# Rotary swap by transfers of SyncE and GpSimd, second tile of V normed later, turns of the identity behind the columns

## The chip, the cores and the metric

The kernel runs on one core of a Trainium2 chip. A core has a matmul engine (TensorE, PE), a vector engine (VectorE, DVE), an activation engine (ScalarE, ACT), GpSimd (POOL) and SyncE (SP), which work at the same time and wait for one another by semaphores. Data lies in on-chip memory (SBUF, 128 partitions), matmul results in eight banks of PSUM. Transfers are issued from an engine's queue and run on 16 DMA engines. The metric is the device time of one execution, in microseconds (us); a tuned kernel counts as faster or slower only where runs of both differ by more than they scatter.

## What is computed

A block of two transformer layers, then a block with another kind of attention, over 256 tokens of width 1024, batch 1, all in float32. Each of the two layers is a gated feed-forward, a mixer and a second feed-forward, with a layer norm behind each. The change touches the mixer, whose core is (cut from the reference):

```python
z = x @ w_in
u, v, q, k, val, gates = jnp.split(z, SPLITS, axis=-1)
u = jax.nn.gelu(u, approximate=False)
v = jax.nn.gelu(v, approximate=False)
h_a = _chunked_sgu(u, v, sgu_ln_g, sgu_ln_b, sgu_w, sgu_b)   # layer norm of v, causal matmul over time, times u
q = _rope(q.reshape(...), cos, sin)
k = _rope(k.reshape(...), cos, sin)
...
def _rope(x, cos, sin):
    x1, x2 = jnp.split(xf, 2, axis=-1)          # halves of 32 channels in each head half of 64
    return jnp.concatenate([x1 * c - x2 * s, x2 * c + x1 * s], axis=-1)
```

The rotary embedding needs, for each channel, its partner 32 channels away. Channels lie on partitions here, so this is a swap of partitions p and p ^ 32. The second block takes time vectors through a modulation (`silu(c) @ w_mod + b_mod`), of which some parts are computed between the steps of the first block.

## The kernel before

Every weight matrix is streamed once. SyncE loads chunks of 1 MB into a ring of three tiles `raw` (function `load`, L634 on; a chunk is loaded when both low halves of the chunk three before it are made). A chunk has two parts of 128 x 1024. For each part ScalarE makes a rounded high half `whi` (L1408) and VectorE, or at layer norms GpSimd, the low half `wlo` = raw - whi (L1861, L2425), in rings of four. A product is then three matmuls (high x high, high x low, low x high), and the order of making halves is that of class `Weights`: `take` makes what is up to four parts ahead, `pass_by(1)` passes one part, `more(k)` makes k parts ahead if the ring has room.

`gemm_a` (L716, L717, L719) has the weights stationary and 256 tokens moving: 8 x 3 = 24 matmuls for a block of 128 output channels. `gemm_b` (L739, L741, L742) has the tokens stationary and 512 weight columns moving.

A mixer goes: the V part by `gemm_b` (8 weight parts), then 16 query and key blocks by `gemm_a` (n = 0 to 15), the gating matmuls (L923, the layer-normed V times the causal matrix), 8 U blocks, then the value part, gates with attention woven in, branches and output.

The rotary, for block n: ScalarE copies the bank to the tile s of the ring `mtmp` (four tiles, L1490). TensorE, one block later, multiplies it by a permutation matrix `perm` into bank 4 or 5 (`rotate`, L904). VectorE multiplies that by the sine into the tile u of the ring (L1974) and s by the cosine into Q or K (L1975). GpSimd adds both (L2484). The order on each engine is that in which its function is written:

```python
                for n in range(16):
                    b = n % 4
                    empty(b)
                    gemm_a(bank[b][:, 0:T], xt, ("qk", l, n))
                    emptied[b] = ((AMX, ("qk", l, n)),)
                    if n:
                        rotate(n - 1)
```

VectorE norms V's two tiles (L1957 to L1967) ahead of these blocks, with GpSimd's power for 1/sqrt (L2477). It adds the bias to the gating result into SG (L1986), which uses banks 6 and 7 in turn.

`mod_columns` (L826) turns a row of the modulation into columns with eight small instructions (four matmuls of 2 columns). `modulation` does the same from sums that VectorE makes, and has one transpose of the identity matrix behind it (`settle`, L774), written to an unused part of the bank, which then carries the signal.

## Time and profile before

| | us |
|---|---|
| median of 3 runs | 1823.71 (1823.33 to 1826.53) |
| the profiled execution | 1826.43 |
| its span | 1824.7 |
| TensorE busy (share of the span) | 1789.1 (98%) |
| VectorE busy | 1136.3 (62%) |
| ScalarE busy | 866.2 (47%) |
| GpSimd busy | 249.4 (14%) |

The span is the time from the first to the last instruction in the profile; 1.7 us lie around it. Matmuls overlap, so the length of one (0.28 us) is more than the time to the next one's start. A transfer is not counted as an engine's busy time.

### The profile page before, as it was taken

The numbers are of one execution on the slowest core, as the hardware profiler recorded it, in microseconds if no ns is written. First come the engines' busy times: TensorE is split into PE (matmuls) and PEld (weight loads), VectorE is DVE, ScalarE is ACT, GpSimd is POOL, SyncE is SP. The second block draws the span as 40 slices with busy tenths as digits, with TensorE's granted clock in tenths as the row PEclk, the third lists the DMA queues.
The fourth block names the chain that finished last, engine by engine and source line by source line (L and its number), as shares of the span: only waits on it lengthen the run. The fifth ranks groups of instructions, "written<-read, shape, count | busy, mean of one in ns | idle before, by whom it ended". The sixth has DMA issues, their size and how long they took to land.

```text
span 1824.7 us, 31051 instructions
## 1 busy us (share of the span) xinstructions
PE 1789.1 (98%) x12824; PEld 1618.3 (89%) x12824; DVE 1136.3 (62%) x1735; ACT 866.2 (47%) x1412; POOL 249.4 (14%) x264
## 2 busy tenths in 40 slices
PE   9999999999999999999999999999999899999998
PEld 8998699999899879997899997999787777889998
DVE  5764686686666466656675776566645555655553
ACT  5453344664445435443435753545345345445443
POOL 2000232121200020002321212000111343100000
PEclk9999999999999999999999999999999999999999
DMA  8565654446566666755745455675553333355553
GB/s 289 188 229 191 227 185 162 162 139 198 195 205 211 208 205 227 238 186 173 260 150 182 140 185 196 222 234 184 172 171 91 95 90 107 116 172 181 188 188 105
DMA packets 252397, 330.58 MB, mean 181 GB/s; under 512 B 13162, under 2 KB 213072, under 8 KB 252256
## 3 DMA queue, kind: packets, MB, share of 16 engines
q1 hardware_dynamic: 248240, 315.31, 53.0%
q0 software_dynamic: 4016, 13.27, 2.1%
q8 instruction: 102, 1.67, 0.4%
q14 instruction: 39, 0.32, 0.0%
HBM read 327.51 MB, written 1.05 MB: 180 GB/s over the span
## 4 chain that ended last, share of the span: by engine, by line
PE 62%; issue 24%; DVE 6%; POOL 3%; ACT 2%; DMA 2%; SPq 0%; POOLq 0%; DVEq 0%; ACTq 0%
PE bank L716 14%; PE bank L719 14%; PE bank L717 14%; PE bank L739 4%; PE bank L741 4%; PE bank L742 4%; DVE X L1939 1%; DMA G<-in_lam_dram 1%; DVE wlo L1861 1%; PE bank L1278 1%; ACT whi L1408 1%; POOL rs L2459 1%; PE bank L1256 1%; PE bank L904 1%; PE bank L942 1%
## 5 line engine op out<-in xcount | busy, mean ns | idle before, releaser
L1861 DVE TENSOR_TENSOR wlo<-raw,whi 128x1024 fp32r<-128x1024 f32 x537 | 664.2, 1241 | 383.6 <-ACT whi L1408 379.7
L1408 ACT ACTIVATE whi<-raw 128x1024 fp32r<-128x1024 f32 x549 | 574.2, 1051 | 390.5 <-PE bank L742 166.1
L716 PE MATMUL bank<-XTh,whi 128*128 128x256 f32 x1984 | 559.9, 282 | 0.0
L719 PE MATMUL bank<-XTh,wlo 128*128 128x256 f32 x1984 | 551.1, 278 | 0.0
L717 PE MATMUL bank<-XTl,whi 128*128 128x256 f32 x1984 | 550.8, 278 | 0.0
L716 PEld LDWEIGHTS bank<-XTh,whi 128*128 128x128 f32 x1984 | 373.4, 188 | 2.9
L717 PEld LDWEIGHTS bank<-XTl,whi 128*128 128x128 f32 x1984 | 374.0, 189 | 1.0
L719 PEld LDWEIGHTS bank<-XTh,wlo 128*128 128x128 f32 x1984 | 372.8, 188 | 0.4 <-DVE wlo L1861 0.3
L716 PE MATMUL bank<-HCh,whi 128*128 128x256 f32 (+1 forms) x880 | 252.4, 287 | 0.6 <-DVE tmp L2355 0.6
L717 PE MATMUL bank<-HCl,whi 128*128 128x256 f32 (+1 forms) x880 | 248.3, 282 | 0.0
L719 PE MATMUL bank<-HCh,wlo 128*128 128x256 f32 (+1 forms) x880 | 248.2, 282 | 0.0
L716 PEld LDWEIGHTS bank<-HCh,whi 128*128 128x128 f32 x880 | 166.1, 189 | 15.7 <-issue 11.4
L717 PEld LDWEIGHTS bank<-HCl,whi 128*128 128x128 f32 x880 | 164.9, 187 | 1.8
L719 PEld LDWEIGHTS bank<-HCh,wlo 128*128 128x128 f32 x880 | 164.8, 187 | 1.7
L2459 POOL TENSOR_TENSOR rs<-rs,half 128x1 f32<-128x1 f32 x12 | 18.3, 1525 | 650.7 <-DVE rs L1933 650.7
L741 PE MATMUL bank<-wlo,ffn1Hh 128*128 128x512 f32 x264 | 102.7, 389 | 0.0
L739 PE MATMUL bank<-whi,ffn1Hh 128*128 128x512 f32 x264 | 102.7, 389 | 0.0
L742 PE MATMUL bank<-whi,ffn1Hl 128*128 128x512 f32 x264 | 102.7, 389 | 0.0
L739 PE MATMUL bank<-whi,XTh 128*128 128x512 f32 x192 | 75.2, 391 | 0.0
L741 PE MATMUL bank<-wlo,XTh 128*128 128x512 f32 x192 | 74.8, 389 | 0.0
L742 PE MATMUL bank<-whi,XTl 128*128 128x512 f32 x192 | 74.7, 389 | 0.0
L742 PEld LDWEIGHTS bank<-whi,ffn1Hl 128*128 128x128 f32 x264 | 49.6, 188 | 10.3
(344 smaller groups left out, 2425.7 us busy)
## 6 DMA issues: line engine op xcount, KB each, us to landing
raw<-in_ffn_w_dram SPq DMA_DIRECT2D x131, 1024.0 KB, 5.1
raw<-in_w_in_dram SPq DMA_DIRECT2D x76, 1024.0 KB, 5.0
raw<-in_w_mod_dram SPq DMA_DIRECT2D x24, 1024.0 KB, 5.1
raw<-in_w_branch_dram SPq DMA_DIRECT2D x16, 1024.0 KB, 4.9
raw<-in_w_out_dram SPq DMA_DIRECT2D x12, 1024.0 KB, 4.8
raw<-in_w_ffn_gate_dram SPq DMA_DIRECT2D x11, 1024.0 KB, 5.2
raw<-in_w_ffn_up_dram SPq DMA_DIRECT2D x11, 1024.0 KB, 5.1
raw<-in_w_ffn_down_dram SPq DMA_DIRECT2D x8, 1024.0 KB, 5.2
```

The source lines that it names most:

```text
L716: e.matmul(o, hi[:, k, w0:w0 + nc_], xh, start=first and k == 0, stop=False)
L717: e.matmul(o, hi[:, k, w0:w0 + nc_], xl, start=False, stop=False)
L719: m = e.matmul(o, lo[:, k, w0:w0 + nc_], xh, start=False, stop=last and k == nk - 1)
L739: e.matmul(o[:, :], xh, hi[:, k, s], start=kk == 0, stop=False)
L741: e.matmul(o[:, :], xh, lo[:, k, s], start=False, stop=False)
L742: m = e.matmul(o[:, :], xl, hi[:, k, s], start=False, stop=kk == nparts * nk - 1)
L904: e.matmul(bank[b][:, 0:T], perm, mtmp[tm[l].slot["s", n]][:, :], start=True, stop=True).then_inc(SMALL.did(("perm", l, n)), 1)
L942: e.matmul(bank[b][:, 0:256], Q[r, h, 128:256], K[r, h, :], start=True, stop=True)
L1256: e.matmul(bank[b][:, :], QNT[r, h // 2, t * 128:(t + 1) * 128], KNT[r, h // 2, :], start=True, stop=True).then_inc(SMALL.did(("ns", u)), 1)
L1408: e.activation(hi_part(n), raw_part(n), ACTF.Copy).then_inc(WHI.did(n), 1)
L1861: e.tensor_tensor(lo_part(n), raw_part(n), hi_part(n).bitcast(F32), ALU.subtract).then_inc(WLO.did(n), 1)
L2459: e.tensor_tensor(rs[:, t, 1:2], rs[:, t, 0:1], nhalf, ALU.pow).then_inc(PLN.did(("rs", j, t)), 1)
```

## The change

- The permutation matrix and its 16 matmuls a layer go. For each block, two transfers on SyncE's queue (rows 0 to 63 of the tile) and two on GpSimd's (rows 64 to 127) copy 32 rows each of s to the swapped place in u. SyncE issues those of two blocks behind each of eight loads; GpSimd's stand in its own loop.
- VectorE multiplies u by the sine in place, in SBUF, two blocks behind the product (`times_sin`), the cosine one block behind. The ring `mtmp` has eight tiles in place of four, and each block its own s and u.
- `norm_v(1)` and GpSimd's power for it are written behind the first query block; ScalarE's and VectorE's `more(1)` ahead of it goes. The loads of the next norm's parameters on GpSimd move to the sixth block.
- `mod_columns` has a turn of the identity behind it, and one stands ahead of the first query block.
- The constants lose 128 columns, so the tiles behind them lie 512 bytes lower.

```diff
--- before.py
+++ after.py
...
-    chunks, on_dve = [], {}
+    chunks, on_dve, first_qk = [], {}, []
...
+        first_qk.append(len(chunks))
...
+        ROT = [signal(f"s_rotary{i}") for i in range(4)]
+        ROTP = [signal(f"s_rotary_pool{i}") for i in range(4)]
...
-        cm, cos, sin, perm = csa[:, 0:256], csa[:, 256:512], csa[:, 512:768], csa[:, 768:896]
+        cm, cos, sin = csa[:, 0:256], csa[:, 256:512], csa[:, 512:768]
...
-            mtmp = some(st, "mtmp", 4, [128, T])
+            mtmp = some(st, "mtmp", 8, [128, T])
...
         tm = []
         for l in range(2):
-            r = Ring(4)
+            r = Ring(8)
             for n in range(16):
-                r.use(("s", n), (SMALL, ("perm", l, n)), (DMX, ("cos", l, n)))
-                if n:
-                    r.use(("u", n - 1), (PMX, ("rot", l, n - 1)))
+                r.use(("s", n), (ROT[n % 4], ("turned", l, n)), (ROTP[n % 4], ("turned", l, n)), (DMX, ("cos", l, n)))
+                r.use(("u", n), (PMX, ("rot", l, n)))
             for n in range(8):
                 r.use(("g", n), (XLO, ("ha", l, n)))
-                if n == 0:
-                    r.use(("u", 15), (PMX, ("rot", l, 15)))
             for n in range(8):
@@ -647,6 +646,15 @@
                 cs = hs[j][1]
                 e.dma_start(dst[:, :, cs], src[:, :, cs]).then_inc(FIRST[j].did(j, by=16), 16)
 
+            def turned(l, n):
+
+
+                ring_free(q, tm[l], ("u", n))
+                q.wait_ge(AMX, ("qk", l, n))
+                for p in (0, 32):
+                    e.dma_start(mtmp[tm[l].slot["u", n]][p:p + 32, :], mtmp[tm[l].slot["s", n]][p ^ 32:(p ^ 32) + 32, :]).then_inc(
+                        ROT[n % 4].did(("turned", l, n), by=16), 16)
+
...
             for c in range(1, before_bias):
                 load(c)
+                for l in range(2):
+                    if first_qk[l] <= c - 4 < first_qk[l] + 8:
+                        for j in range(2):
+                            turned(l, 2 * (c - 4 - first_qk[l]) + j)
...
                 for j in range(4):
-                    mm = e.matmul(bank[b][:, 2 * j:2 * j + 2], spare[0:m, j * 128:(j + 1) * 128], cmb[0:m, :], start=True, stop=True)
-                mm.then_inc(MOD.did(("columns", g)), 1)
+                    e.matmul(bank[b][:, 2 * j:2 * j + 2], spare[0:m, j * 128:(j + 1) * 128], cmb[0:m, :], start=True, stop=True)
+                settle(b).then_inc(MOD.did(("columns", g)), 1)
                 emptied[b] = ((DMD, g),)
@@ -897,21 +909,13 @@
                 for b in range(4, 8):
                     emptied[b] = ((AMX, ("V", l, (b - 4) // 2, b % 2)),)
 
-                def rotate(n):
-                    b = 4 + n % 2
-                    q.wait_ge(AMX, ("qk", l, n))
-                    empty(b)
-                    e.matmul(bank[b][:, 0:T], perm, mtmp[tm[l].slot["s", n]][:, :], start=True, stop=True).then_inc(
-                        SMALL.did(("perm", l, n)), 1)
-                    emptied[b] = ((DMX, ("sin", l, n)),)
-
+                empty(3)
+                settle(3)
                 for n in range(16):
                     b = n % 4
                     empty(b)
                     gemm_a(bank[b][:, 0:T], xt, ("qk", l, n))
                     emptied[b] = ((AMX, ("qk", l, n)),)
-                    if n:
-                        rotate(n - 1)
                 for g2 in range(4):
                     b = 6 + g2 % 2
                     q.wait_ge(DMX, ("v", l, 1))
@@ -928,8 +932,6 @@
                     empty(b)
                     gemm_a(bank[b][:, 0:T], xt, ("u", l, n))
                     emptied[b] = ((AMX, ("u", l, n)),)
-                    if n == 0:
-                        rotate(15)
...
@@ -1479,8 +1481,6 @@
                     if t:
                         w.more(3)
                     q.wait_ge(MM, ("V", l, t))
-                    if t:
-                        w.more(1)
                     for c in range(2):
                         e.activation(V[:, t, c * 512:(c + 1) * 512], bank[4 + 2 * t + c][:, :], ACTF.Gelu).then_inc(AMX.did(("V", l, t, c)), 1)
@@ -1949,9 +1949,7 @@
             def mixer(l):
                 w.pass_b(8, 3)
                 w.more(3)
-                for t in range(2):
-                    if t:
-                        w.more(1)
+                def norm_v(t):
                     for c in range(2):
                         q.wait_ge(AMX, ("V", l, t, c))
                         e.bn_stats(st6[:, t, c, :], V[:, t, c * 512:(c + 1) * 512]).then_inc(DMX.did(("stats", l, t, c)), 1)
...
-                def rotate(n):
-                    b, dst, j, scale = 4 + n % 2, (Q, K)[n // 8], n % 8, (0.125, 1.0)[n // 8]
-                    u = mtmp[tm[l].slot["u", n]]
-                    q.wait_ge(SMALL, ("perm", l, n))
-                    ring_free(q, tm[l], ("u", n))
-                    e.scalar_tensor_tensor(u[:, :], bank[b][:, 0:T], scale, sin, ALU.mult, ALU.mult).then_inc(DMX.did(("sin", l, n)), 1)
+                def times_cos(n):
+                    dst, j, scale = (Q, K)[n // 8], n % 8, (0.125, 1.0)[n // 8]
+                    q.wait_ge(AMX, ("qk", l, n))
                     e.scalar_tensor_tensor(dst[:, j, :], mtmp[tm[l].slot["s", n]][:, :], scale, cos, ALU.mult, ALU.mult).then_inc(
                         DMX.did(("cos", l, n)), 1)
 
+                def times_sin(n):
+                    u, scale = mtmp[tm[l].slot["u", n]], (0.125, 1.0)[n // 8]
+                    q.wait_ge(ROT[n % 4], ("turned", l, n))
+                    q.wait_ge(ROTP[n % 4], ("turned", l, n))
+                    e.scalar_tensor_tensor(u[:, :], u[:, :], scale, sin, ALU.mult, ALU.mult).then_inc(DMX.did(("sin", l, n)), 1)
+
+                norm_v(0)
                 for n in range(16):
                     w.pass_by(1)
+                    if n == 0:
+                        norm_v(1)
                     if n:
-                        rotate(n - 1)
+                        times_cos(n - 1)
+                    if n > 1:
+                        times_sin(n - 2)
+                times_cos(15)
                 q.wait_ge(MIN[l], "in")
                 for g in range(8):
...
                 for n in range(8):
                     w.pass_by(1)
-                    if n == 0:
-                        rotate(15)
-                    else:
+                    if n < 2:
+                        times_sin(14 + n)
+                    if n:
                         low("ha", HAl, HAh, n - 1, mtmp[tm[l].slot["g", n - 1]])
                 low("ha", HAl, HAh, 7, mtmp[tm[l].slot["g", 7]])
@@ -2472,29 +2479,43 @@
                                 channel_multiplier=1).then_inc(PMX.did(("ws", l)), 1)
                 w.pass_b(8, 3)
                 w.more(3)
-                for t in range(2):
+
+                def power(t):
                     q.wait_ge(DMX, ("var", l, t))
                     e.tensor_tensor(rs[:, t, 1:2], rs[:, t, 0:1], nhalf, ALU.pow).then_inc(PMX.did(("rs", l, t)), 1)
-                q.wait_ge(DMX, ("v", l, 1))
-                load_gb((2, 6)[l], I["ln_g"][l, 1], I["ln_b"][l, 1])
-
+
+                power(0)
                 def rotate(n):
                     dst, j = (Q, K)[n // 8], n % 8
+                    q.wait_ge(DMX, ("sin", l, n))
                     q.wait_ge(DMX, ("cos", l, n))
                     e.tensor_tensor(dst[:, j, :], dst[:, j, :], mtmp[tm[l].slot["u", n]][:, :], ALU.add).then_inc(PMX.did(("rot", l, n)), 1)
 
+                def turned(n):
+                    ring_free(q, tm[l], ("u", n))
+                    q.wait_ge(AMX, ("qk", l, n))
+                    for p in (64, 96):
+                        e.dma_start(mtmp[tm[l].slot["u", n]][p:p + 32, :], mtmp[tm[l].slot["s", n]][p ^ 32:(p ^ 32) + 32, :]).then_inc(
+                            ROTP[n % 4].did(("turned", l, n), by=16), 16)
+
                 for n in range(16):
                     w.pass_by(1)
-                    if n:
-                        rotate(n - 1)
+                    turned(n)
+                    if n == 0:
+                        power(1)
+                    if n > 1:
+                        rotate(n - 2)
+                    if n == 5:
+                        q.wait_ge(DMX, ("v", l, 1))
+                        load_gb((2, 6)[l], I["ln_g"][l, 1], I["ln_b"][l, 1])
                 for n in range(8):
                     w.pass_by(1)
                     s = mtmp[tm[l].slot["g", n]]
                     q.wait_ge(AMX, ("u", l, n))
                     q.wait_ge(DMX, ("sg", l, n))
                     e.tensor_tensor(s[:, :], s[:, :], SG[:, n, :], ALU.mult).then_inc(PMX.did(("a", l, n)), 1)
-                    if n == 0:
-                        rotate(15)
+                    if n < 2:
+                        rotate(14 + n)
                 w.pass_b(8, 2)
```

TensorE, from the last product of V (512 columns) to the first query block of layer 0. Before:

```order
L741 MATMUL bank<-wlo,XTh 128x512
L742 MATMUL bank<-whi,XTl 128x512
L716 MATMUL bank<-XTh,whi 128x256
L717 MATMUL bank<-XTl,whi 128x256
L719 MATMUL bank<-XTh,wlo 128x256
```

After:

```order
L753 MATMUL bank<-wlo,XTh 128x512
L754 MATMUL bank<-whi,XTl 128x512
L788 MATMUL bank<-cst 128x128
L728 MATMUL bank<-XTh,whi 128x256
L729 MATMUL bank<-XTl,whi 128x256
L731 MATMUL bank<-XTh,wlo 128x256
```

The turn of the identity stands between them.

VectorE in layer 0, from the last operation of V's norm on; wlo is the low half of a weight part. Before:

```order
L1963 SCALAR_TENSOR_TENSOR XTf<-XTf,mv,gb 128x1024
L1967 SCALAR_TENSOR_TENSOR XTf<-XTf,rs,gb 128x1024
L1861 TENSOR_TENSOR wlo<-raw,whi 128x1024
L1974 SCALAR_TENSOR_TENSOR mtmp<-bank,csa 128x256
L1975 SCALAR_TENSOR_TENSOR Q<-mtmp,csa 128x256
```

After:

```order
L1961 SCALAR_TENSOR_TENSOR XTf<-XTf,mv,gb 128x1024
L1965 SCALAR_TENSOR_TENSOR XTf<-XTf,rs,gb 128x1024
L1861 TENSOR_TENSOR wlo<-raw,whi 128x1024
L1970 SCALAR_TENSOR_TENSOR Q<-mtmp,csa 128x256
L1861 TENSOR_TENSOR wlo<-raw,whi 128x1024
L1970 SCALAR_TENSOR_TENSOR Q<-mtmp,csa 128x256
L1977 SCALAR_TENSOR_TENSOR mtmp<-mtmp,csa 128x256
```

The norm and the first low half stand where they did; the sine product reads mtmp in place of a bank, and comes one low half later than its cosine.

SyncE, the loads of the first mixer's V, query and key weights. Before:

```order
L642 DMA raw<-in_w_mod_dram 128x4x512 x2
L642 DMA raw<-in_w_in_dram 128x2x1024 x4
L642 DMA raw<-in_w_in_dram 128x8x256 x12
L642 DMA raw<-in_w_in_dram 128x2x1024 x4
L642 DMA raw<-in_w_in_dram 128x8x256 x8
```

After:

```order
L641 DMA raw<-in_w_mod_dram 128x4x512 x2
L641 DMA raw<-in_w_in_dram 128x2x1024 x4
L641 DMA raw<-in_w_in_dram 128x8x256 x5
L655 DMA mtmp<-mtmp 32x256 x4
L641 DMA raw<-in_w_in_dram 128x8x256
```

Behind the fifth load of `chunk_a` weights, and each of the seven that follow, stand four transfers of 32 rows.

## Rows read from the trace of the kernel before

**Rows 1.** The page: busy us, share of the span and instructions of each engine.

```profile
PE 1789.1 (98%) x12824; PEld 1618.3 (89%) x12824; DVE 1136.3 (62%) x1735; ACT 866.2 (47%) x1412; POOL 249.4 (14%) x264
```

**Rows 2.** Timeline, TensorE, first layer: start us, length us, line, tiles, idle before.

```profile
230.97 0.28 PE L716 MATMUL bank<-XTh,whi 128*128 128x256 f32 x1
...
283.55 0.83 PE L923 MATMUL bank<-G,XTf 128*128 128x128 f32 x6
...
287.32 0.37 PE L716 MATMUL bank<-XTh,whi 128*128 128x256 f32 x1
...
310.36 0.40 PE L739 MATMUL bank<-whi,XTh 128*128 128x512 f32 x1
```

**Rows 3.** One line's instructions, L904: ns shortest/median/longest, first and last start us.

```profile
L904 PE MATMUL bank<-mtmp,csa x64: 377/377/454, 236.6 to 949.7; 128*128 128x256 f32 x64
```

**Rows 4.** Timeline, TensorE, around one turn of the rotary.

```profile
247.55 0.59 PE L904 MATMUL bank<-mtmp,csa 128*128 128x256 f32 x2
247.79 0.47 PE L716 MATMUL bank<-XTh,whi 128*128 128x256 f32 x1
248.10 0.28 PE L717 MATMUL bank<-XTl,whi 128*128 128x256 f32 x1
```

**Rows 5.** Timeline, all engines, the wait inside the query blocks, first layer.

```profile
242.52 1.22 DVE L1861 TENSOR_TENSOR wlo<-raw,whi 128x1024 fp32r<-128x1024 f32 x1
242.93 0.28 PE L719 MATMUL bank<-XTh,wlo 128*128 128x256 f32 x1
243.65 0.42 DVE L1974 SCALAR_TENSOR_TENSOR mtmp<-bank,csa 128x256 f32<-128x256 f32 x1
244.22 0.67 PE L904 MATMUL bank<-mtmp,csa 128*128 128x256 f32 x2 [1.01 <-DVE mtmp L1974]
```

**Rows 6.** Windows, TensorE: stretch us, its length, busy (x matmuls), clock, DMA share, GB/s.

```profile
472.50:475.50 3.00, 2.72 (x12) 0.50 1.09 396
478.00:564.00 86.00, 86.00 (x732) 1.00 0.64 206
567.00:599.00 32.00, 32.00 (x284) 1.00 0.61 197
1640.00:1756.00 116.00, 116.00 (x987) 1.00 0.58 184
```

**Rows 7.** Timeline, TensorE, columns of a modulation and the identity turn behind (L776).

```profile
564.62 1.84 PE L806 MATMUL bank<-sel,sums 128*128 128x2 f32 x16
566.33 0.31 PE L776 MATMUL bank<-cst 128*128 128x128 f32 x1
566.39 0.37 PE L716 MATMUL bank<-XTh,whi 128*128 128x256 f32 x1
```

**Rows 8.** Timeline, TensorE, two rows of columns (L826) with no turn behind.

```profile
472.78 0.58 PE L701 MATMUL bank<-XTh,whi 128*128 128x256 f32 x1 [0.43 <-DVE XTl L1888]
...
1636.57 1.05 PE L826 MATMUL bank<-cmb,spare 2*128 2x2 f32 x8
1637.55 0.38 PE L716 MATMUL bank<-HCh,whi 128*128 128x256 f32 x1
```

**Rows 9.** DMA issues: tile<-source, queue, count, KB each, median us to landing.

```profile
gb<-in_ln_b_dram POOLq DMA_DIRECT2D x6, 512.0 KB, 8.2
BT<-in_na_rpb_dram SPq DMA_DIRECT2D x16, 96.0 KB, 7.4
out_dram<-OUT SPq DMA_DIRECT2D x4, 256.0 KB, 2.1
SO<-in_gla_w_alpha_dram POOLq DMA_DIRECT2D x2, 16.0 KB, 3.4
```

**Rows 10.** GpSimd: one line's instructions (L2539), then groups by line, 230 to 310 us.

```profile
L2539 POOL DMA_DIRECT2D SO<-in_gla_w_alpha_dram x2: 495/506/518, 1354.2 to 1354.7; - x2
L2484 POOL TENSOR_TENSOR Q<-Q,mtmp 128x256 f32<-128x256 f32 x8 | 10.5, 1310 | 8.2 <-DVE Q L1975 8.2
L2484 POOL TENSOR_TENSOR K<-K,mtmp 128x256 f32<-128x256 f32 x8 | 6.8, 849 | 17.8 <-DVE K L1975 17.8
```

More of the change, by code:

```diff
@@ L32 @@
 C_ID, C_SHARED, C_CM = 0, 128, 128
-C_COS, C_SIN, C_PERM, C_FIRST = 384, 640, 896, 1024
+C_COS, C_SIN, C_FIRST = 384, 640, 896
 C_COSG, C_SING, C_PERMG, C_SCAN, C_GM, C_IN, C_NEG, C_CMB, C_ALL = (
-    1024, 1280, 1536, 1664, 2432, 2688, 2944, 3200, 3202)
+    896, 1152, 1408, 1536, 2304, 2560, 2816, 3072, 3074)
 R_GB, R_DG, R_C, R_CC, R_N1, R_N2, R_BM, R_BA, R_GN, R_NQ, R_NK, R_ALL = (
@@ L278, in plan @@
     parts = [(c, j) for c in range(len(chunks)) for j in range(len(chunks[c][3]))]
-    return chunks, parts, whole, on_dve, before_bias
+    return chunks, parts, whole, on_dve, before_bias, first_qk
 MOVES, STANDS = 48, 0
@@ L381, in program @@
     with ctx:
-        chunks, parts, whole, on_dve, before_bias = plan(I)
+        chunks, parts, whole, on_dve, before_bias, first_qk = plan(I)
         of_chunk = {}
```

3 lines of the change are left out of this document (1 added, 2 removed).

## The prediction

> **What bounds the kernel now.** I read the page first, then TensorE's timeline in the part of the mixer that the diff touches, then windows for its pace, then who waits for whom, and the landing times of DMAs last. TensorE is busy 98% of the span, VectorE 62%, GpSimd 14% [rows 1]. So a saving counts almost one for one if it is taken from TensorE's own instructions, and anything put on the other engines costs nothing until it makes TensorE wait. The reader is to see three things in TensorE's rows.
>
> First, the swap of the rotary halves is a matmul of its own between two blocks of 24 products, and on the chip it is two instructions, 64 for both layers [rows 3]. One swap starts at 247.55, the block behind it at 247.79, and the second product of that block only at 248.10 [rows 4]. Second, TensorE has two paces at the same granted clock of 1.00, the upper of its two levels (2.4 GHz): 86 us for 732 products is 117.5 ns each, 116 us for 987 the same, but 32 us for 284 is 112.7 ns [rows 6]. The pace stays over whole blocks and changes where something else stands between them: it was slow until 564, and behind the columns and one turn of the identity it is fast [rows 6, 7]. A block of 24 takes 2.82 us slow and 2.70 us fast by these windows; I use 2.72 for the fast one, since a window counts the products cut by its edges. Third, in the query blocks TensorE waits once a layer: a product ends its issue at 242.93, the next instruction starts at 244.22, of which 1.01 us is idle, waiting for VectorE [rows 5].
>
> **The touched stretch, before.** The first layer's 16 query and key blocks begin at 230.97, the gating matmuls at 283.55, the 8 U blocks at 287.32, and the next stage at 310.36 [rows 2]: 79.4 us for 24 blocks. The second layer has the same 16 swaps [rows 3] and I give it the same sum.
>
> **Swaps removed.** Without a swap the product at 248.10 would stand where two steps of 0.12 from the last product of the block before would put it: 247.43 (0.12 before 247.55) plus 0.24 is 247.67. So a swap costs 0.43 us, and 32 of them 13.8 us [rows 3, 4]. All of it is on TensorE, none hidden.
>
> **The wait at the fifth block.** By the order the small work on VectorE is where it was: norm of both tiles of V, then the low half of the fifth block's weights, which starts at 242.52 and ends at 243.74 [rows 5]. The later place of the second norm in the source therefore moves nothing on VectorE, and I give it 0. Before, TensorE waited there for the sine product of swap 0 (a bank). That wait goes, but the low half is late next: four blocks at 2.72 behind 231.15 end at 242.0, the third product of the fifth needs the low half at 242.3 and gets it at about 243.8. A wait of 1.5 replaces one of 1.2 (244.22 less the 0.12 that follows 242.93 anyway): cost 0.3 a layer.
>
> **Turns of the identity.** One before the query blocks and one behind each of the seven columns. Behind columns the turn starts at 566.33, the product at 566.39, its successor 0.21 later by the next start: about 0.15 to 0.2 us each [rows 7]. Five of the nine stand where TensorE then idles 0.43 us for XTl [rows 8] or in the V stage's start, so I count 4 x 0.2 = 0.8 us. What they may bring is the fast pace. The U blocks take 23.04 us with one swap among them, (23.04 - 0.43) / 8 = 2.83 each; the query blocks 52.58 with 15 swaps and the wait of 1.2, (52.58 - 6.45 - 1.2) / 16 = 2.81 each [rows 2]: nearly all slow. All 24 fast would be 24 x 0.10 less the few that are fast, 2.0 us a layer. But the wait at the fifth block can end the fast pace, so I take 1.4 a layer, with 0.4 and 2.0 as ends. The last feed-forward is slow in its window behind the columns [rows 6, 8]: 987 products x 4.8 ns are 4.7 us. Its turn would stand directly ahead of the products, as in rows 7, so I take 4.0 (ends 0 and 5.7, should the down products gain too). The feed-forward from 478 on is slow too, 732 x 4.8 = 3.5 us, but there TensorE idles between turn and products, and two others that are fast now could become slow: 0.5 gained, from -3 to +3.5. A stretch at the clock's lower level (1.2 GHz) shows too, 12 products in 3.0 us where 26 would go [rows 6]; whether such stretches move with the timing I can't say, some 1.4 us each, value 0.
>
> **What takes the swap's place.** For each block two transfers of 32 rows on SyncE's queue, two on GpSimd's, then the sine product on VectorE and the sum on GpSimd, both one block later than before. TensorE waits for none of it directly: only for the eviction (ring of 8 tiles, so for block n-4's transfers), for the low halves that VectorE makes between these products, and for SG behind the last block. The bounds come from the nearest rows. On SyncE's queue: 2.1 us from issue to landing for the output with little ahead of it, 7.4 for small rows issued right behind a 1 MB load [rows 9]; the even blocks' transfers stand just so behind a load, so I take 6 for them and 3 for the odd. On GpSimd's: 3.4 for 16 KB, 8.2 for a broadcast [rows 9]; I take 3.4, and about 8 for the one block behind the gb loads. Issue on GpSimd is 0.51 each [rows 10], and a sum 0.74 to 1.65 us (means 0.85 and 1.31 in rows 10), so GpSimd works 1.0 + 0.85 to 1.65 = 1.9 to 2.7 of each 2.72 us.
>
> The Trainium skill (SBUF — State Buffer, "Who interferes with whom") says a VectorE instruction with two SBUF inputs and a GpSimd instruction that reads SBUF block each other. The sine product read PSUM before and reads SBUF now, so by that rule more of the sums would take the long form; the means in rows 10 agree that there are two forms. No term rests on it.
>
> VectorE's order is low half n+3, cosine n-1, sine n-2. After block n ends, its sine comes up 5.8 us later (two blocks, 0.4); a landing of 6 delays it by under 1 us and the low halves are made three blocks ahead, 8 us, so the query blocks don't feel it. SyncE holds no load: its transfers wait for blocks done before the load could go. At the end VectorE has the last low half, cosine and sine before it adds the eight SG; if it is late there, the gating matmuls wait, since they use two banks. With GpSimd at 2.7 of 2.72 the delay behind the gb loads is not worked off and VectorE comes some 4 us late; with sums of 0.85 it is worked off and under 1 us remains. I take 1.7 a layer, 0.3 and 4.5 as ends.
>
> **The sum.** -13.8 (swaps) + 0.6 (waits) + 0.8 (turns) - 2.8 (pace in the mixers) + 3.4 (late VectorE) - 4.0 (last feed-forward) - 0.5 (other paces) = -16.3. The profiled execution took 1826.43 us (span 1824.70), so about 1810.1. The median of the runs, 1823.71, is 2.7 lower; the profiled one is as long as the slowest of them. Taken from the median it is 1807.4. I say 1808.
>
> **Rivals.**
> - Late transfers but still a gain: 4.5 us a layer at SG and one more microsecond in the blocks, +7.6 on the forecast: 1815. For it: GpSimd's 2.7 of 2.72. Against it: the sums whose VectorE neighbour reads PSUM or idles are short.
> - The turns do nothing for the pace: no 2.8, 4.0, 0.5: 1815. For it: the turn in rows 7 is one kind of place; behind 512-column products nothing shows it. Against: slow before and fast after it.
> - Slower: GpSimd's own round sets the pace. Its transfers for block n+1 are issued after the sum of n-2, which waits for the sine, which waits for the landing of n-2: three blocks last 8.2 us, and the round is landing + 0.5 (second issue) + 0.4 (sine) + 1.65. It decides from a landing of 5.6 us on. With the broadcast's 8.2 [rows 9] the round is 10.8, 0.85 a block too long, 13 blocks: 11 a layer, 22 in all, in place of the 3.4: 1808 + 19 = 1827. For it: 8.2 is what this queue shows beside loads. Against: those are 512 KB, ours 32 KB, and the 16 KB ones landed in 3.4.
> - The change doesn't do what it says: the second norm of V is not later on VectorE; that part is 0 in the sum already.
>
> **Chances.** Forecast 0.55 (own range 1802 to 1812), late transfers 0.20, no pace 0.18, slower 0.05, faster than 1800 0.02. Range 1799 to 1818. A measurement of this kernel tells 0.2%, 3.6 us, from no change: faster 0.93, same 0.03, slower 0.04.
>
> **What would show it.** No swap on TensorE; from the first query block to the stage behind U 71 to 74 us instead of 79.4; a wait of about 1.5 us at the fifth block for the low half; the gating matmuls within 5 us; landings of the 32-row transfers near 6 and 3.4 us; windows of 112.7 ns a product in the query blocks and after the last columns. Wrong if TensorE waits for low halves in later query blocks, if the gating matmuls last over 8 us, or if windows in the last feed-forward still read 117.5.

## The result, and the profile after

The changed kernel takes 1830.19 us (median of 20 runs) where the kernel before takes 1822.99 beside it (20 runs): ratio 1.0039, 95% interval 1.0027 to 1.0050. It is slower by 0.4%, and the forecast of 1808 us was wrong by 22. The profiled execution has a span of 1828.5 us against 1824.7.

The page: TensorE has 9 us less to do than in [rows 1] and GpSimd 38 us more; VectorE as much as before.

```profile
PE 1779.8 (97%) x12769; PEld 1608.1 (88%) x12769; DVE 1138.2 (62%) x1735; ACT 866.7 (47%) x1412; POOL 287.5 (16%) x328
```

TensorE's timeline, the landmarks of [rows 2] in the first layer, and the gating of the second (start us, length us, line, what it does, idle before and who ended it):

```profile
230.22 0.37 PE L728 MATMUL bank<-XTh,whi 128*128 128x256 f32 x1
...
243.03 0.39 PE L731 MATMUL bank<-XTh,wlo 128*128 128x256 f32 x1 [1.44 <-DVE wlo L1861]
...
268.03 0.39 PE L731 MATMUL bank<-XTh,wlo 128*128 128x256 f32 x1 [2.14 <-DVE wlo L1861]
...
280.74 1.95 PE L927 MATMUL bank<-G,XTf 128*128 128x128 f32 x16
285.80 3.57 PE L927 MATMUL bank<-G,XTf 128*128 128x128 f32 x16 [3.12 <-DVE SG L1993]
289.13 0.37 PE L728 MATMUL bank<-XTh,whi 128*128 128x256 f32 x1
...
310.98 0.40 PE L751 MATMUL bank<-whi,XTh 128*128 128x512 f32 x1
...
932.44 0.39 PE L731 MATMUL bank<-XTh,wlo 128*128 128x256 f32 x1 [3.67 <-DVE wlo L1861]
...
943.22 1.95 PE L927 MATMUL bank<-G,XTf 128*128 128x128 f32 x16
949.53 3.78 PE L927 MATMUL bank<-G,XTf 128*128 128x128 f32 x16 [4.36 <-DVE SG L1993]
```

No swap is left, and yet the stretch from the first query block to the stage behind U takes 310.98 - 230.22 = 80.8 us, against 79.4 [rows 2]; in the second layer 82.2. The expected wait is there, 1.44 us at the fifth block. Not expected are the wait for low halves at block 12 counted from zero, which the expectations call the twelfth (2.14 and 3.67 us), and the wait inside the gating matmuls for VectorE's sums of the gate (3.12 and 4.36): the gating takes 8.4 us, and 9.7 in the second layer, where it took 3.8 [rows 2]. Behind three of these four long waits TensorE also runs at the lower of its two levels for a while; behind the one of 3.67 us at 932.44 it doesn't. TensorE's windows (stretch, its length, busy (x matmuls), granted clock, DMA share, GB/s):

```profile
231.00:241.00 10.00, 10.00 (x91) 1.00 0.71 231
...
268.00:272.00 4.00, 3.97 (x20) 0.57 0.35 84
285.00:289.00 4.00, 3.20 (x15) 0.57 0.36 125
932.40:936.40 4.00, 3.96 (x34) 1.00 0.16 37
947.00:955.00 8.00, 5.47 (x27) 0.57 0.43 149
```

Twenty products in 4 us where some 35 go at full clock: about 1.7 us lost in the first of these stretches, beside the wait that stands ahead of it, and by the lengths of the three some 6 us in all (an estimate).

Who made VectorE late is read ahead of the wait at 268.03, in the other engines' timeline of the first layer:

```profile
245.21 3.79 POOL L2492 TENSOR_TENSOR Q<-Q,mtmp 128x256 f32<-128x256 f32 x1 [2.70 <-DVE mtmp L1977]
...
257.16 0.37 SPq L641 DMA_DIRECT2D raw<-in_w_in_dram  x1
257.62 0.57 POOL L2437 DMA_DIRECT2D gb<-in_ln_g_dram  x1
257.62 2.46 SPq L655 DMA_DIRECT2D mtmp<-mtmp  x4
258.19 0.54 POOL L2438 DMA_DIRECT2D gb<-in_ln_b_dram  x1
258.71 1.01 POOL L2498 DMA_DIRECT2D mtmp<-mtmp  x2
...
262.17 0.95 DVE L1970 SCALAR_TENSOR_TENSOR Q<-mtmp,csa 128x256 f32<-128x256 f32 x1
266.41 0.42 DVE L1977 SCALAR_TENSOR_TENSOR mtmp<-mtmp,csa 128x256 f32<-128x256 f32 x1 [3.29 <-DMA mtmp<-mtmp]
266.48 0.38 ACT L1490 ACTIVATE mtmp<-bank 128x256 f32<-128x256 f32 x1 [5.11 <-DMA mtmp<-mtmp]
266.75 1.22 DVE L1861 TENSOR_TENSOR wlo<-raw,whi 128x1024 fp32r<-128x1024 f32 x1
```

Block 6, counted from zero as all numbered blocks from here on, is evicted by 251.7 (its landings are read from the same trace's DMA events). SyncE issues its two transfers at 257.62, behind a weight load; GpSimd its two at 258.71, behind the two loads of the layer norm's rows. They land at 264.2 and 266.3. VectorE's sine for this block stands in its queue for 3.29 us, and behind it stands the low half for which TensorE waits at 265.9 to 268.0. From eviction to landing it is 14.6 us; I had counted two blocks. The first row is the addition of block 0. It takes 3.79 us where such additions took 1.66 at most in the kernel before, beside VectorE products with both inputs in SBUF that follow one another until 248.4, and the transfers of block 3, evicted at 241.8, stand behind it in GpSimd's queue until 248.95. The waits of the first layer's stretch (engine, line, who is waited for, total us, times, longest):

```profile
DVE mtmp L1977 <- DMA mtmp<-mtmp: 8.8, 4, 3.3
ACT mtmp L1490 <- DMA mtmp<-mtmp: 8.1, 2, 5.1
...
PE bank L731 <- DVE wlo L1861: 3.8, 3, 2.1
...
PE bank L927 <- DVE SG L1993: 3.1, 1, 3.1
```

Elsewhere the two traces differ as follows, from the start of one row of columns to the next: from the last columns to TensorE's last product it is 178.9 us instead of 183.8, the part from 472 on takes 196.0 instead of 197.9, but the one behind it 200.0 instead of 196.5, and the one ahead of the last columns 311.1 instead of 307.0.

The clock differs over the whole kernel. In windows of 0.5 us the changed kernel's profile has eight stretches at the lower level, 40 us in all, the kernel before four, 15.5 us. The mean granted clock is 0.990 in the median of the changed kernel's 20 runs, and 0.994 in that of 29 runs of the kernel before, taken beside own_half below. Worked out from these two means, up to 7 us lie in the clock, as much as the whole slowdown (an estimate; some of that time is idle).

### The profile page after: what moved, and what is told of

It reads as the page before. It is cut to its first block, busy times and chain, and to the rows that moved or that the text cites. A ratio compares the mean times of both kernels' runs of the same rounds, so it can differ in the third digit from the quotient of the medians.

```text
span 1828.5 us, 31151 instructions
## 1 busy us (share of the span) xinstructions
PE 1779.8 (97%) x12769; PEld 1608.1 (88%) x12769; DVE 1138.2 (62%) x1735; ACT 866.7 (47%) x1412; POOL 287.5 (16%) x328
## 3 DMA queue, kind: packets, MB, share of 16 engines
q8 instruction: 101, 1.65, 0.4%
## 4 chain that ended last, share of the span: by engine, by line
PE 59%; issue 25%; DVE 8%; DMA 3%; POOL 3%; ACT 2%; SPq 0%; POOLq 0%; DVEq 0%; ACTq 0%
PE bank L728 13%; PE bank L731 13%; PE bank L729 12%; PE bank L751 4%; PE bank L753 4%; PE bank L754 4%; DMA mtmp<-mtmp 2%; DVE wlo L1861 1%; DVE X L1939 1%; PE bank L1280 1%; POOL rs L2466 1%; ACT whi L1410 1%; PE bank L1258 1%; DMA G<-in_lam_dram 1%; PE bank L944 1%
## 5 line engine op out<-in xcount | busy, mean ns | idle before, releaser
L1861 DVE TENSOR_TENSOR wlo<-raw,whi 128x1024 fp32r<-128x1024 f32 x537 | 656.7, 1227 | 383.8 <-ACT whi L1410 378.8
```

The lines of the kernel that those rows point to most:

```text
L1861: e.tensor_tensor(lo_part(n), raw_part(n), hi_part(n).bitcast(F32), ALU.subtract).then_inc(WLO.did(n), 1)
```

## The experiments

Theory A: the transfers land late and VectorE, which works in order, passes that on. Rivals: VectorE is too busy for a block of 2.7 us without any transfer; the turns of the identity cost what they bring. Ratios are against the kernel before, run beside each kernel.

**own_half**: the changed kernel without its transfers.

```
-  turned(...)                       # SyncE and GpSimd
-  q.wait_ge(ROT...); q.wait_ge(ROTP...)
-  sine: u <- u * sin
+  sine: u <- s * sin
```

> The changed kernel without its 64 transfers: the sine product reads the unswapped columns, so the rotation is left out of the result. Theory A (VectorE stands behind transfers that land late, and with it the low halves and the gate's sums, so that TensorE waits at the twelfth block and in the gating): no sine waits, the two stretches fall from 80.8 and 82.2 us to 71 to 75, the kernel to 1811 to 1818 us. Theory B (VectorE has too much to do for a query block of 2.7 us, with or without transfers): it stays over 1825.

Measured 1806.52 us, 0.9906 (0.9885 to 0.9927). TensorE's timeline:

```profile
231.09 0.36 PE L727 MATMUL bank<-XTh,whi 128*128 128x256 f32 x1
...
276.43 1.95 PE L926 MATMUL bank<-G,XTf 128*128 128x128 f32 x16
278.62 2.05 PE L926 MATMUL bank<-G,XTf 128*128 128x128 f32 x16 [0.24 <-DVE SG L1992]
...
302.28 0.40 PE L750 MATMUL bank<-whi,XTh 128*128 128x512 f32 x1
```

302.28 - 231.09 = 71.2 us, in both layers: 9.6 and 11.0 less than with transfers, 20.6 in all. Query blocks give 5.2 and 4.5 of it, the gating 4.4 and 5.7, the U blocks 0 and 0.8. The kernel is faster than the 1811 to 1818 us expected, the stretches as theory A says. So everything that the swaps were to give was there, and transfers took it back. VectorE without them keeps the pace, with a wait of 0.24 us at the gate: the first rival is out as a cause by itself.

**gb_late**: the two loads that stood ahead of block 6's transfers, moved.

```
-  if n == 5: load_gb(...)           # GpSimd, in the query loop
+  load_gb(...)                      # behind the last addition
```

> The changed kernel with GpSimd's two loads of the layer norm's rows moved from behind its sixth block to behind the last addition. Theory A1 (these loads, directly ahead of the transfers of a block, make the landing of over 8 us on which the eviction waits 5 us and the twelfth block 2.4 and 3.9 us): those waits go, with the stretch of half clock behind them, 4 to 8 us less, 1822 to 1826 us. Rival A2 (GpSimd's and SyncE's transfers land late by themselves, in an in-order round): within 1.5 us of the changed kernel.

Measured 1822.50, 0.9994 (0.9978 to 1.0010): 0.0045, some 8 us, under the changed kernel, as A1 said. The wait at block 12 is gone (0.5 us is left earlier in the second layer), but the stretches are still 78.0 and 78.8 us, since the wait at the gate has grown:

```profile
PE bank L927 <- DVE SG L1993: 4.9, 1, 4.9
```

**add_one** and **gb_add_one**: GpSimd's additions of one column, in the changed kernel and in gb_late.

```
-  e.tensor_tensor(dst[:, j, :], dst[:, j, :], u[:, :], ALU.add)
+  e.tensor_tensor(dst[:, j, 0:1], dst[:, j, 0:1], u[:, 0:1], ALU.add)
```

> The changed kernel with GpSimd's 32 additions cut to one column each, so the sum is left out of the result; the transfers and all waits stay. Theory C (VectorE's cosine product takes 0.95 us instead of 0.41 to 0.62 because GpSimd's addition runs beside it, and GpSimd issues its transfers 1.4 us late for the same addition): the cosine falls to about 0.5 us, the waits for low halves shrink, 4 to 10 us less than the changed kernel. Theory A alone (landings): less than 3 us.

> gb_late with GpSimd's additions cut to one column each (the sum is left out of the result). Theory C (VectorE's lateness at the gate is its missing slack: cosine 0.96 instead of 0.42 beside an addition): cosines at 0.42, round 1.8 us, the wait at the gate under 0.5 us, stretches at 71.5 to 73, 9 to 12 us under gb_late. Rival A (landings alone): the wait at the gate stays over 2 us.

Measured 1822.39, 0.9983 (0.9965 to 1.0002), and 1816.22, 0.9940 (0.9918 to 0.9961). The cosine product of the K blocks in the changed kernel, and in gb_add_one (ns shortest/median/longest):

```profile
L1970 DVE SCALAR_TENSOR_TENSOR K<-mtmp,csa x8: 412/954/971, 267.9 to 284.7; 128x256 f32<-128x256 f32 x8
```

```profile
L1970 DVE SCALAR_TENSOR_TENSOR K<-mtmp,csa x8: 415/418/421, 264.2 to 279.6; 128x256 f32<-128x256 f32 x8
...
DVE mtmp L1977 <- DMA mtmp<-mtmp: 10.7, 5, 3.0
...
PE bank L927 <- DVE SG L1993: 3.3, 1, 3.3
```

The long form of the cosine is the addition's doing. add_one is some 10 us under the changed kernel by the ratios, as theory C says, but only 4 of it lie in the stretches (79.1 and 79.9), and the waits at block 12 have grown to 3.8 and 4.5 us. In gb_add_one the gate still waits 3.3 us with VectorE's round at 1.8 us instead of 2.35: VectorE now waits 10.7 us for transfers instead of 5.9. The kernel is some 10 us under gb_late, 3.1 of it in the two stretches, but theory C alone falls. GpSimd's timeline in gb_add_one shows what stands ahead of its transfers:

```profile
263.22 1.10 POOL L2492 TENSOR_TENSOR Q<-Q,mtmp 128x1 f32<-128x1 f32 x1 [2.23 <-ACT mtmp L1490]
264.26 1.01 POOL L2498 DMA_DIRECT2D mtmp<-mtmp  x2
265.29 0.84 POOL L2492 TENSOR_TENSOR Q<-Q,mtmp 128x1 f32<-128x1 f32 x1
266.07 1.01 POOL L2498 DMA_DIRECT2D mtmp<-mtmp  x2
...
280.07 0.20 POOL L2492 TENSOR_TENSOR K<-K,mtmp 128x1 f32<-128x1 f32 x1
```

The transfers of block 10 go out at 266.07, behind the addition of block 7, whose sine came at 264.52; they land at 272.3. SyncE's, issued at 266.62, land last, at 273.0, and block 10's sine starts at 272.98. So three blocks take 8.46 us by this round, and 8.16 on TensorE. The round is closed by both queues and not by GpSimd's alone: its transfers landed 0.7 us before SyncE's, and in four of the five waits of the sine in this layer SyncE's landed last.

**slim**: transfers of 16 columns instead of 256.

```
-  e.dma_start(u[p:p + 32, :], s[p ^ 32:(p ^ 32) + 32, :])
+  e.dma_start(u[p:p + 32, 0:16], s[p ^ 32:(p ^ 32) + 32, 0:16])
```

> gb_late with each of the 128 transfers cut to 16 of 256 columns (2 KB instead of 32 KB; the sine reads the unswapped tile, so the rotation is left out of the result), all waits in place. Theory E1 (a landing of 6.3 us is the time of getting through behind a 1 MB weight load and of the transfers' own setup, whatever their size): the landing stays over 5 us and the time within 3 us of gb_late. Theory E2 (it is their own bytes, 1 KB in each of 32 rows): landings of 2 to 3 us and 5 us or more less.

Measured 1810.50, 0.9951 (0.9933 to 0.9970). The time from issue to landing of all transfers in 229 to 300 us, first gb_late, then slim:

```profile
DMA to landing us min/median/max: 1.7/4.3/5.8
```

```profile
DMA to landing us min/median/max: 1.5/3.9/5.4
```

A sixteenth of the bytes takes 0.4 us off; from a block's first issue to its last landing it is still 5.5 to 6.0 us (blocks 8 and 10), against 6.2 to 6.4. The time is getting through, not size (E1). E1's price was wrong, though. The kernel is about 8 us under gb_late and the stretches are some 3 and 4 us shorter (75.2 and 74.4). In the first layer the four waits of the sine that gb_late has at blocks 2, 3, 6 and 10 fall from 1.7, 1.8, 1.1 and 1.3 us to 1.5, 0.7, 0.2 and 0.6, and the gate's from 4.9 to 2.6. That the same gain is paid in each round is my reading; it is not tested by itself.

**ring12**: six blocks in flight instead of four.

```
-  r = Ring(8)
+  r = Ring(12)                      # 4 more tiles in P
```

> gb_late with one more edit: 12 tiles instead of 8 for the evictions and the turned halves (4 lie in a buffer of the attention that is idle here), so six blocks are in flight instead of four. In gb_late the transfers of block 10 are issued at 266.90 on both queues, 4 us behind their eviction, and land at 273.3; those of block 14 at 277.75 and 283.4: the tile comes free only when the addition four blocks back is done. Theory D (a closed round through the ring: issue, landing 6.3 us, sine, addition, next issue, 10.7 us for four blocks): with six blocks the transfers go out right behind the eviction, the sines no longer wait, VectorE comes 3 to 5 us earlier to the gate's sums; 3 to 7 us under gb_late. Rival C (VectorE's own full round of 2.35 us is what is late): the wait at the gate stays over 4 us, within 2 us of gb_late.

Measured 1817.22, 0.9991 (0.9978 to 1.0004): the same as gb_late, stretches of 78.1 and 78.6. Transfers of block 10 still go out at 267.06 on both queues, on SyncE's directly behind a load at 266.59. The ring is not what holds them; theory D falls, and the gate's waits of 4.5 and 4.7 us are as rival C says. With gate_first's edit on top, **ring12_gate** took 1812.11, 0.9949 (0.9932 to 0.9967), not below gate_first.

**sync_first**: SyncE's transfers ahead of the load that stood ahead of them.

```
-  load(c)
   turned(...); turned(...)
+  load(c)
```

> gb_late with SyncE's transfers of each pair of blocks ahead of the weight load that now stands ahead of them. In gb_late the load of 266.44 waits for a low half that ends at 266.36, and the transfers of block 10, evicted at 262.9, go out at 266.9 behind it. Theory F (SyncE's in-order queue closes a round: low half, load, transfers, landing, sine, next low half): the transfers go out within 1 us of the eviction, land without a new 1 MB load directly ahead, sine waits fall under 2 us; 3 us or more under gb_late. Rival G (GpSimd's transfers, as late as SyncE's, hold the sine just as well, or the loads now come too late): within 2 us or slower.

Measured 1821.11, 0.9977 (0.9957 to 0.9998), an interval that overlaps gb_late's: some 3 us better by the ratios, but not clear of noise. The stretches are 75.3 and 78.7 us. In gb_late, around block 10, evicted at 262.9:

```profile
265.15 1.21 DVE L1861 TENSOR_TENSOR wlo<-raw,whi 128x1024 fp32r<-128x1024 f32 x1
...
266.44 0.37 SPq L641 DMA_DIRECT2D raw<-in_w_in_dram  x1
266.90 1.00 POOL L2498 DMA_DIRECT2D mtmp<-mtmp  x2
266.90 1.17 SPq L655 DMA_DIRECT2D mtmp<-mtmp  x2
```

The load waits for the low half to end at 266.36, and the transfers wait behind the load. With the swap they go out at 264.5, 1.5 us behind their eviction, and SyncE's transfers land in 2.9 us in the median of the kernel instead of 4.4. But the sine waits 6.4 us in all, where it waited 5.9, now for GpSimd's: block 10's go out at 266.79, 3.8 us behind the eviction. So the load ahead is one of two holds on a block's transfers (F for SyncE's, G for the time), and without the first alone the second layer's stretch gains nothing.

**gate_first** and **cos_bank**: two ways to give VectorE room, each on gb_late. The first puts three cosines and four sines behind the sums of the gate; the second reads the cosine's columns from PSUM.

```
-  for n in 1..15: times_cos(n - 1), times_sin(n - 2)
+  for n in 1..13: times_cos(n - 1), times_sin(n - 2)   # rest with the U blocks
```

```
-  cosine: dst <- s * cos
+  cosine: dst <- bank[n % 4] * cos
```

> gb_late with one more edit: the last three blocks' cosines and four blocks' sines (and their additions) behind the gate's sums instead of ahead of them. VectorE reaches the sums 3 cosines and 2 sines, about 3.9 us, earlier: the wait at the gate falls from 5.2 us to about 1.5, and the stretch of half clock behind it may go too. 3 to 5 us per mixer, 1813 to 1817 us. Rival: the late rotary pieces make the low halves of the U blocks late, and the wait only moves: within 3 us of gb_late.

> gb_late with one more edit: the cosine product reads its columns from the PSUM bank and not from SBUF. In gb_late VectorE's round is 2.35 us long and never idle from 263 us on (low half 1.21, cosine 0.96, sine 0.41), so it cannot win back what it lost to transfers, and TensorE waits 5.2 us for the gate's sums. Theory C (the cosine takes 0.96 us because both its inputs and both of GpSimd's addition lie in SBUF): with one input in PSUM it takes about 0.5, the wait at the gate falls to under 1.5 us, the time is 6 to 10 us under gb_late, 1812 to 1817. Rival: the cosine stays at 0.9 or more, wherever its input is, or VectorE only waits for transfers instead: within 3 us of gb_late.

Measured 1813.10, 0.9931 (0.9904 to 0.9957), and 1814.08, 0.9938 (0.9917 to 0.9960). gate_first's wait at the gate is 2.6 us instead of 4.9, its stretches 75.2 and 74.5. Both are clear of gb_late, by some 11 and 10 us in the ratios; 7 and 5.6 us of that lie in the stretches. In cos_bank the cosine is short throughout, with the additions whole beside it:

```profile
L1970 DVE SCALAR_TENSOR_TENSOR K<-bank,csa x8: 409/414/418, 262.0 to 277.4; 128x256 f32<-128x256 f32 x8
...
DVE mtmp L1977 <- DMA mtmp<-mtmp: 7.9, 6, 2.0
...
PE bank L927 <- DVE SG L1993: 1.4, 1, 1.4
```

The addition of block 0, 3.79 us in the changed kernel, takes 1.65. The first layer's stretch falls to 73.8 us, the second's to 77.5 with a wait of 4.6 at the gate. VectorE's slack matters, next to the landings and not in their place.

**act_issue**: ScalarE issues GpSimd's transfers, on gb_late.

```
-  turned(n) on GpSimd
+  turned(n) on ScalarE, behind its eviction of block n
```

> gb_late with one more edit: ScalarE issues the two transfers of the upper partitions, right behind its own eviction, and GpSimd only adds. Theory A3 (GpSimd's in-order round, 1.0 us of issue and 1.4 us of addition, makes these transfers and the additions late): the sine waits less, the additions keep up, 3 to 8 us under gb_late. Rival: the transfers land just as late behind the weights' loads, or ScalarE's evictions now stand behind its own transfers: within 3 us or slower.

Measured 1819.40, 0.9965 (0.9943 to 0.9987), 5 us under gb_late by the medians' ratios but with overlapping intervals; the stretches are 77.9 and 78.4. The sine waits fall from 5.9 to 3.3 us, but ScalarE is now late with the high halves: VectorE waits for them 8.6 us instead of 6.7, the last eviction ends 3 us behind its block, and the gate waits 4.6. One wait turned into another.

**combo** (gate_first, cos_bank and act_issue), **gate_cos_last** (gate_first and cos_bank, one turn of the identity only) and **best_sync_first** (that with sync_first):

> gb_late with the edits of cos_bank, gate_first and act_issue together. If the waits are causes in a row (landing, VectorE's full round, gate), all of them go: both stretches at 71 to 73 us as without transfers, 1806 to 1811 us. If one of them is only moved, 1812 or more.

> gate_first and cos_bank together, GpSimd issuing as in the changed kernel, with one turn of the identity only. ScalarE's issues stood in its own way in combo (gaps of 0.9 and 0.5 us in the U blocks), so this may be as good or better: ratio 0.990 to 0.993. If the waits at the gate are over 2 us here, GpSimd's in-order issue matters and it is 0.994 or more.

> The same swap on SyncE's queue in gate_cos_last (ratio 0.9922 so far). By theory F the remaining sine waits shrink but TensorE hardly waited for them there: 0 to 2 us under gate_cos_last. If the later loads starve the weights: slower than gate_cos_last by 2 us or more.

Measured 1810.40, 0.9923 (0.9896 to 0.9950); 1812.77, 0.9922 (0.9891 to 0.9953); 1813.89, 0.9951 (0.9928 to 0.9973). combo with one turn (combo_last) took 1814.09, 0.9925 (0.9901 to 0.9950). combo's stretches are 75.0 and 73.8 us, not the 71 to 73 that its expectation has if all waits go. combo, gate_cos_last and combo_last beat the kernel before by some 14 us and the changed one by more; nothing tells the three apart. gate_cos_last's first layer, TensorE:

```profile
231.02 0.28 PE L728 MATMUL bank<-XTh,whi 128*128 128x256 f32 x1
...
276.99 4.02 PE L925 MATMUL bank<-G,XTf 128*128 128x128 f32 x32
...
304.64 0.40 PE L751 MATMUL bank<-whi,XTh 128*128 128x512 f32 x1
```

All 32 gating matmuls are one row, without a wait, and both stretches take 73.6 us. In best_sync_first the sines wait 0.3 us in all, but nothing is gained by it: TensorE no longer waited for them, and all its 32 query blocks run at the slow pace (118 ns a product).

**turns_only**, **no_turns** and **turn_last**: the turns of the identity added to the kernel before, taken from the changed one, and added to the kernel before in one place alone.

```
-  mm.then_inc(MOD.did(("columns", g)), 1)
+  settle(b).then_inc(...)           # turns_only; turn_last: only for g == 11
+  settle(3)                         # turns_only: ahead of the query blocks
```

> The kernel before with only the turns of the identity added (behind the columns and ahead of the query blocks); swap by TensorE as it was. My forecast priced the pace at 4.5 us outside the mixers and 2.8 us in them; by that theory this kernel takes 1816 to 1819 us. Rival: the paces of the stages only change places from program to program (in the changed kernel two stages turned fast and two slow), and the time is within 2 us of the kernel before.

> The changed kernel without the turns of the identity. My forecast priced them at 7.3 us of pace less 0.8 of their own: by that this kernel would take 6 us more, 1836 us. The kernel before with the turns alone gained 1.5 us with an interval that holds zero; by that rival this one is within 3 us of the changed kernel.

> The kernel before with one turn of the identity only, behind the last columns, ahead of the last feed-forward. In all profiles with that turn the time from the last columns to the end is 178.7 us, in both without it 183.5. Theory P1 (this turn makes the last feed-forward fast, the other turns only shuffle paces): 4 to 5 us under the kernel before, about 0.9975 as a ratio. Rival P2 (profile-to-profile paces, no effect of its own): within 1.5 us.

Measured 1822.65, 0.9990 (0.9973 to 1.0008); 1823.94, 1.0022 (1.0004 to 1.0041); 1822.93, 0.9975 (0.9959 to 0.9991). The last feed-forward, 1650 to 1756 us, in the kernel before and in turn_last:

```profile
1650.00:1756.00 106.00, 106.00 (x902) 1.00 0.59 187
```

```profile
1650.00:1756.00 106.00, 106.00 (x937) 1.00 0.62 196
```

117.5 against 113.1 ns a product. In the profiles of all 18 kernels with a turn behind the last columns it is 178.9 us from the start of these columns to the end of TensorE's last product, in the kernel before and no_turns 183.8 (the expectation above counts 178.7 and 183.5, with the same difference). So this one turn is worth its 4.8 us (P1), and turn_last gains 4.6 by its ratio. All turns together gain 1.8 us with an interval that reaches past no change: in turns_only the profile has 4.1 us won in the part from 472 on and 2.6, 4.9 and 2.7 lost in three of the parts behind it. But turn_last, whose instructions are those of the kernel before up to the last columns, differs from it by as much there (2.5 and 1.4 won, 5.0 and 2.6 lost), so such shifts come without any turn. Taken from the changed kernel, all turns together make it no slower. Why one stage is fast and another slow stays open, and so does why the last turn works.

## Why the prediction was wrong

- **Swaps removed (-13.8)**: right. Without transfers the stretches are 71.2 us, 8.2 less each; 6.9 of that is the swaps by the forecast, the rest pace less the wait; no run prices the swaps apart from the pace.
- **Wait at the fifth block (+0.6)**: right, 1.44 us of idle in the first layer as forecast and 1.03 in the second; the second norm of V moved nothing.
- **Pace in the mixers (-2.8)**: a gain of about this size came, but not by the turn. Nine of the first layer's 16 query blocks and twelve of the second's run at 113 ns a product. In own_half, with the turn ahead of them, the first four blocks of each layer are slow and the twelve behind the wait at the fifth are fast, and in gate_cos_last, with no turn there, it is the same. Its windows, in the first four blocks and behind them:

```profile
232.00:242.00 10.00, 10.00 (x88) 1.00 0.69 230
250.00:260.00 10.00, 10.00 (x91) 1.00 0.85 264
```

Over all kernels without swaps the first four blocks were fast behind a turn in 4 of 26 mixers, without one in none of 8. With the turns and the swaps, in turns_only, both stretches take 79.4 us as before. I had the wait at the fifth block as what could end the fast pace; the fast pace begins behind it. The lower clock level behind three of the long waits (at 268, 285 and 947 us) cost some 6 us that the sum had at 0.
- **Last feed-forward (-4.0)**: right, -4.8. **Other paces (-0.5)** and turns (+0.8): all that lies ahead of the last columns and outside the two stretches came to +5.7 us of TensorE's time, +3.5 and +4.1 the largest parts. Stretches at the lower level are 10 us longer there than in the kernel before, at half the speed some 5 us (an estimate). Whether the longer waits in the mixers bring them about is not shown.
- **What takes the swap's place (+3.4)**: this step failed. The stretches came out at 80.8 and 82.2 us where the forecast has 73.1, 16.8 of the 20 us between forecast and profile. The sentence was "After block n ends, its sine comes up 5.8 us later ... so the query blocks don't feel it. SyncE holds no load". I took landings of 6, 3 and 3.4 us and counted them from the end of a block. In the trace they are counted from the issue, and the issue comes late: on SyncE behind a load that waits for VectorE's low half, on GpSimd behind the addition three blocks back and once behind the loads of the norm's rows. Eviction to landing is 10.2 us for block 10 and 14.6 for block 6. Landings on GpSimd's queue were 4.1 us in the median of the first layer's stretch, near my 3.4, but 5.9 to 7.6 for blocks 3, 6 and 10, which a sine waited for; the one number I had for a small transfer there came from a stretch without this traffic. And one addition took 3.79 us, more than the 0.74 to 1.65 I had for all, which sent block 3's transfers out late. I saw both orders in the code and checked only whether transfers hold the load, not whether the load holds the transfers.
- **The rival** "GpSimd's own round sets the pace", decided from a landing of 5.6 us, got 0.05. The mechanism that it names is there: a block's transfers stand in order behind the addition of an earlier block, which waits for a sine, which waits for a landing. But it is not GpSimd's round alone. Of the four waits of the sine in the changed kernel's first layer two end with GpSimd's landing and two with SyncE's, and in gb_add_one the round of 8.46 us for three blocks ends with SyncE's. Its price came out by another sum: the round is only 0.1 a block longer than TensorE's, and most of the loss is a few waits of the sine (8.8 us in the first layer) that VectorE, with a round of 2.35 in TensorE's 2.72, can't work off before the gate, plus the lower clock level behind them. Where the slack went the cosines show: 954 ns beside an addition with both inputs in SBUF, 414 with one in PSUM. The Trainium skill (SBUF — State Buffer, "Who interferes with whom") says that a VectorE instruction with two SBUF inputs contends with a GpSimd instruction that reads SBUF. The trace agrees by these two numbers, and by the addition of 3.79 us that is 1.65 in cos_bank. I had cited it and said that no term rests on it; by cos_bank's ratio it is worth about 10 us, 5.6 of them in the two stretches.
- "The turns do nothing" (0.18) was right for all turns but the last, as far as the runs show.

## What to carry to other kernels

When a step inside an engine is replaced by a transfer between engines, count from the producer's end to the consumer's start: what stands ahead of the issue in each issuing queue (and what that waits for), the landing beside this stage's own traffic, and then the next round, since a lateness that feeds its own cause is paid in every round. Before adding work to an engine that runs ahead of TensorE, compare its round with TensorE's: with 0.4 us of slack a block, a wait of 3 us stands for eight blocks. When such a change disappoints, first take the suspected wait away whole (own_half), which told in one run that the gain was there to be had, and then look at what stands behind it on the waiting engine: reordering two pieces of work (gate_first) shortened the stretches as much as faster transfers did (slim: 149.5 us for the two, gate_first 149.7).

## What the runs showed of the hardware that was not expected

- Transfers of 32 rows inside SBUF land in 1.7 us at best and 4.3 in the median beside 1 MB loads; with a sixteenth of the bytes 3.9.
- A VectorE product of 128x256 takes 0.95 us beside a GpSimd addition if both its inputs are in SBUF, and 0.41 if one is in PSUM, with the same additions running.
- A GpSimd addition of one column takes 0.20 us on its timeline at 280.07 in gb_add_one, but 0.84 to 1.10 beside VectorE's low halves, which have both inputs in SBUF, and 3.24 where VectorE's products follow one another without a gap; of 256 columns 0.74, 1.38 to 1.65 and 3.79. The time is the wait for VectorE and not the columns.
- SyncE's transfers of 32 rows land in 4.4 us in the median of gb_late and in 2.9 in sync_first, where they no longer stand directly behind a load.
- One turn of the identity behind the last columns (eight small instructions) sets the pace of the next thousand products: 113 instead of 117.5 ns, with the same 178.9 us to TensorE's end in 18 of 18 profiles, against 183.8 in the two without it. Behind the turn ahead of the query blocks the next four blocks were fast in 4 of 26 mixers, and in none of 8 without it.
- After the waits of 2.14, 3.12 and 4.36 us in the changed kernel TensorE was granted the lower level (windows at 0.57 in the mean); behind the wait of 3.67 us, and behind those of 1.44 and 1.03 at the fifth block, it was not.
